# Two hybrid mixers on one core: narrow projection columns appended to wider units, and the second mixer's units reordered

## Chip, cores, metric

One core of one Trainium2 chip. The metric is the device time of one launch in microseconds (us); lower is better.

## What is computed

A stack of four layers on 256 tokens of width 1024, in float32. The two layers of the first kind are half a gated feed-forward block, a hybrid mixer and another half block; the two of the second kind are a hybrid mixer and a feed-forward block with squared ReLU; a norm ends the stack. Cut to the parts that matter here:

```python
def hybrid_mixer(h, w_in, ...):                       # first kind, two layers
    dn_qkv, dn_z, dn_b, dn_a, sb_q, sb_k, sb_v, gate_a, gate_b = split_cols(h @ w_in)
    ...
    beta = jax.nn.sigmoid(dn_b.astype(jnp.float32)).transpose(0, 2, 1)
    g = (-jnp.exp(a_log.astype(jnp.float32))
         * jax.nn.softplus(dn_a.astype(jnp.float32) + dt_bias.astype(jnp.float32))).transpose(0, 2, 1)

def hybrid_layer(x, positions, g_mix, w_in, ...):     # second kind, two layers
    h = rms_norm(x, g_mix)
    (a_q, a_k, a_v, b_qlat, b_kvlat, b_krope,
     c_q, c_k, c_v, c_f, d_val, d_gate) = jnp.split(h @ w_in, split_points, axis=-1)
    ...
    k_rot = apply_rope(b_krope, positions)
    log_f = jax.nn.log_sigmoid(c_f.astype(jnp.float32) + b_forget.astype(jnp.float32))
```

Three outputs of the projections are narrow: `dn_b` and `dn_a` together (16 columns), `c_f` (4 columns) and `b_krope` (32 columns). The three attentions of the second mixer have four heads each.

## The kernel before

**Units.** All weights are read as units of 2048 numbers on each of 128 partitions: 1024 rows by 256 columns (as eight chunks of 128 rows), or 256 rows by 1024 columns. SP loads a unit into one of three `raw` buffers; ScalarE rounds it into `whi` (`split_hi`), VectorE writes the rest into `wlo` (`split_lo`); TensorE multiplies in three products, high by high, high by low and low by high (`product3`). A buffer's next load waits for `lo_done`, its next rounding for `multiplied`. Each engine's program is written out by hand, unit after unit; on ScalarE and VectorE the split of unit n+2 stands ahead of the work on unit n's result.

**Two layouts.** In `feature_product` the weights are stationary and the 256 tokens move: the result has features on the rows, 48 products of 256 columns a unit. In `row_unit` (the value units `sv`, `av`, `cv`) the tokens are stationary, 128 at a time, and the weights move: the result has tokens on the rows.

**Borders.** A mixer begins at a border: the last rows of the block before are added to x (L424), squared (L519 to L531), the scale is taken (L535), x scaled (L550, L556) and turned by TensorE (`norm_pe`, L573); chunk by chunk ScalarE writes `xhi` (L546) and VectorE `xlo` (L561), and `chunk_ready` holds TensorE until a chunk has both. VectorE splits the mixer's first unit ahead of the border.

**First mixer** (`mix1_*`): 28 projection units (`IN1`, from `sk` 0), then gates, branches and output. Ahead of unit 0 the 16 columns are multiplied by themselves, `ba_hi` and `ba_lo` stationary, the 256 tokens moving, chunk by chunk (24 products); the 16-row result is copied (L1097), turned back in two transposes (L964) and copied again, and `small_act_1` and `small_dve_1` work on it at unit 2, the cumulative sum follows at unit 4.

**Second mixer** (`mix2_*`): ten projection units (`IN2`), 16 gate units, four branch units, four output units. The 4 columns of `c_f` are multiplied ahead of unit 0 in the same way (`cf_hi`, `cf_lo`). The 160 columns of `b_kvlat` and `b_krope` are taken as one unit, bkv, whose two products overlap by 64 columns. Latent norms, up projections and the rotary turn follow at fixed units. Head i of the twelve has its scores on TensorE at the end of unit 7 + i (`HEAD2_AT`), its maximum on VectorE and its exponential on ScalarE at 8 + i, its weights scaled by VectorE (L2326 to L2329) and turned by TensorE (L2097) at 9 + i, its values at 10 + i. VectorE's rotary steps (`rope_dve`, L2289 to L2301) stand in unit 7, `mask_rows_dve` in unit 8, `sums_dve` in unit 10, and the 31 taps of a convolution (L2413, L2415) are spread over the units by `TAPS_AT`.

```python
TAPS_AT = {7: 4, 8: 4, 9: 4, 10: 3, 11: 3, 12: 3, 13: 2, 14: 2, 15: 2, 16: 2, 17: 1, 18: 1}
```

Of the kernel before, what the change touches and what calls it, by code (L numbers as in the profile page):

```python
# [6 lines left out]
F32 = mybir.dt.float32  # L7
# [27 lines left out]
ARENA = 19840  # L35
# [25 lines left out]
def constants():  # L61
# [5 lines left out]
    for s in range(LOW, LEVELS):  # L67
        parts[f"level{s}"] = (r >> (s + 1) == c >> (s + 1)) & (c >> s & 1 == 1) & (r >> s & 1 == 0)
    b = np.arange(BLK)
# [11 lines left out]
def constants_2():  # L81
# [12 lines left out]
    parts = {"ones2": np.ones((P, T)), "causal": np.where(r > c, MASKED, 0.0),  # L94
# [13 lines left out]
def hybrid_stack_kernel(nc, d, out):  # L108
    ctx = ExitStack()
    with ctx:  # L110
# [8 lines left out]
        raw = [sb(f"raw{s}", [P, UNIT]) for s in range(SLOTS)]  # L119
        whi = [sb(f"whi{s}", [P, UNIT], F32R) for s in range(SLOTS)]  # L120
        wlo = [sb(f"wlo{s}", [P, UNIT], F32R) for s in range(SLOTS)]
# [41 lines left out]
        small = sb("small", [P, 256])  # L163
        later_keys = sb("later_keys", [P, 384])
        ba_w = (sb("ba_raw", [P, KC, 16]), sb("ba_hi", [P, KC, 16], F32R), sb("ba_lo", [P, KC, 16], F32R))
# [10 lines left out]
        def as_in(w):  # L176
            return w[:].rearrange("p (c n) -> p c n", c=KC)

        def as_out(w):
            return w[:].rearrange("p (c n) -> p c n", c=2)  # L180
# [45 lines left out]
        tensor_waited = sem("tensor_waited")  # L226
# [61 lines left out]
        def split_lo(e, n):  # L288
            s, r = n
            e.wait_ge(hi_done[s], r)  # L290
            e.wait_ge(raw_in[s], r * 16)
            e.tensor_tensor(wlo[s][:], raw[s][:], whi[s][:].bitcast(F32), ALU.subtract).then_inc(lo_done[s], 1)  # L292
# [479 lines left out]
        def ffn1_dve(e, l, r0, u0, j, f):  # L772
# [59 lines left out]
            split_lo(e, unit(r0, u0 + U_FFN1))  # L832
# [9 lines left out]
        N1 = len(IN1)  # L842
        CONV = [n for n in range(N1) if IN1[n][0] in ("q", "k", "v")]
# [28 lines left out]
        ba_turn = sg[0][0:16, 0:T]  # L872
# [4 lines left out]
        ba_raw, ba_hi, ba_lo = ba_w  # L877

        def ev(name, per):
# [4 lines left out]
            ba_hi_done=1, ba_lo_done=1, ba_product=1, ba_copied=1, ba_turned=1, ba_kept=1, exp_b=1, one_b=1, beta_done=1, a_shift=1, abs_a=1,  # L884
# [12 lines left out]
        V["ba_lo_done"].start = 1  # L897
# [4 lines left out]
        def mix1_sync(e, l, r0, u0):  # L902
# [5 lines left out]
            e.wait_ge(V["ba_lo_done"].sem, 1 + l)  # L908
            e.dma_start(ba_raw[:], w[l, :, BA_COL:BA_COL + 16].rearrange("(c p) n -> p c n", p=P)).then_inc(ba_in.sem, 16)
            for n in range(N1):  # L910
                kind, g = IN1[n]
                load_unit(e, unit(r0, u0 + n), columns(w, KIND_COL[KINDS.index(kind)] + g * 256), as_in, True)
# [24 lines left out]

        def head_at(n, after):

            return HEAD_AT.index(n - after) if n - after in HEAD_AT else None  # L940

        def mix1_pe(e, l, r0, u0, j):
            norm_pe(e, j)

            e.wait_ge(*V["ba_hi_done"](l))
            e.wait_ge(*V["ba_lo_done"](l))
            for c in range(KC):
                chunk_ready(e, j, c)
                mm = product3(e, bank[4][0:16, 0:T], ba_hi[:, c, :], ba_lo[:, c, :], xhi[:, c, :], xlo[:, c, :],
                              c == 0, c == KC - 1)  # L950
            mm.then_inc(V["ba_product"].sem, 1)
            for n in range(N1 + TAIL):
                if n < N1:
                    if n >= 2:
                        kept_unit(e, l, n - 2)
                    if IN1[n][0] == "sv":
# [3 lines left out]
                if n == 1:  # L960
                    e.wait_ge(*V["ba_copied"](l))
                    e.sem_inc(tensor_waited)
                    for t in range(TT):
                        mm = e.transpose(bank[4][:, t * 16:(t + 1) * 16], ba_turn[:, t * P:(t + 1) * P], ident[0:16, 0:16])  # L964
                    mm.then_inc(V["ba_turned"].sem, 1)
                if n == 4:
# [102 lines left out]
        def keep_unit_act(e, l, r0, u0, n):  # L1069
            kind, g = IN1[n]  # L1070
            wait_unit(e, r0, u0, n)
            if n in CONV:
# [3 lines left out]
                e.activation(pre[i % 2][:, :, 3:3 + T], b2(n % 2), ACT.Copy).then_inc(V["pre_copied"].sem, 1)  # L1076
            elif kind == "sv":
                e.activation(sv[:, :, g * 256:(g + 1) * 256], b2(n % 2), ACT.Copy).then_inc(V["kept"].sem, 1)
            else:
                e.activation(home(n), bank[n % 2][:], ACT.Copy).then_inc(V["kept"].sem, 1)  # L1080

        def mix1_act(e, l, r0, u0, j):
            split_hi(e, unit(r0, u0))
            e.wait_ge(ba_in.sem, l * 16 + 16)
            e.wait_ge(multiplied[(u0 - 4) % SLOTS], r0 + (u0 - 4) // SLOTS + 1)
            e.activation(ba_hi[:], ba_raw[:], ACT.Copy).then_inc(V["ba_hi_done"].sem, 1)
            norm_act(e, j, lambda c: col("mix_norm", l, c), unit(r0, u0 + 1))
            for n in range(N1 + TAIL):
# [4 lines left out]
                if n + 2 <= N1 + 1:  # L1093
                    split_hi(e, unit(r0, u0 + n + 2))
                if n == 0:
                    e.wait_ge(*V["ba_product"](l))
                    e.activation(ba_turn, bank[4][0:16, 0:T], ACT.Copy).then_inc(V["ba_copied"].sem, 1)  # L1097
# [4 lines left out]
                if n == 5:  # L1102
# [5 lines left out]
                if n == 2:  # L1108
# [81 lines left out]
        def mix1_dve(e, l, r0, u0, j):  # L1190
            e.wait_ge(*V["ba_hi_done"](l))
            e.tensor_tensor(ba_lo[:], ba_raw[:], ba_hi[:].bitcast(F32), ALU.subtract).then_inc(V["ba_lo_done"].sem, 1)
            xlo_dve(e, j, lambda c: col("mix_norm", l, c))
            split_lo(e, unit(r0, u0 + 1))
            for n in range(N1 + TAIL):
# [12 lines left out]
                if n + 2 <= N1 + 1:  # L1208
# [5 lines left out]
                if n == 5:  # L1214
# [29 lines left out]
                if n == 2:  # L1244
# [61 lines left out]
        def small_act_1(e, l):  # L1306
            e.wait_ge(*V["ba_turned"](l))
            e.activation(ba, bank[4][:, 0:32], ACT.Copy).then_inc(V["ba_kept"].sem, 1)
            e.wait_ge(*V["ba_kept"](l))
# [375 lines left out]
        def mix1_delta_dve(e, l, r0, u0):  # L1685
# [27 lines left out]
            for s in range(LOW, LEVELS):  # L1713
                mask = const(f"level{s}").unsqueeze(1).to_broadcast([P, 4, P])
                last = s == LEVELS - 1
                for g in range(GROUPS):
                    e.wait_ge(*V["m_product"](l, (s - LOW) * 4 + g))
                    if last:
                        e.tensor_tensor(Mb[g][:, :, 64:P], b4(g)[:, :, 64:P], mask[:, :, 64:P], ALU.mult)\
# [72 lines left out]
        CF_COL = 1952  # L1792
# [7 lines left out]
        TAPS_AT = {7: 4, 8: 4, 9: 4, 10: 3, 11: 3, 12: 3, 13: 2, 14: 2, 15: 2, 16: 2, 17: 1, 18: 1}  # L1800
# [22 lines left out]
        cf_turn = rtmp[0:H2, 0:T]  # L1823
# [9 lines left out]
        def const2(name):  # L1833
# [5 lines left out]
        cf_raw, cf_hi, cf_lo = [w[:, :, 0:H2] for w in ba_w]  # L1839
# [7 lines left out]
            cf_hi=1, cf_lo=1, cf_product=1, cf_copied=1, cf_turned=1, cf_kept=1, cf_abs=1, cf_exp=1, cf_ln=1, lf=1,  # L1847
# [10 lines left out]
        def mix2_sync(e, l, r0, u0, j):  # L1858
            w = d["w_in_2"]

            def columns(w, c):
# [4 lines left out]
            e.dma_start(ba_w[0][:, :, 0:H2], w[l, :, CF_COL:CF_COL + H2].rearrange("(c p) n -> p c n", p=P))\  # L1866
             .then_inc(small_in, 16)
# [4 lines left out]
            for n in range(10):  # L1872
                load_unit(e, unit(r0, u0 + n), columns(w, IN2_COL[IN2[n]]), as_in, True)
# [78 lines left out]
        def mix2_pe(e, l, r0, u0, j):  # L1952
            norm_pe(e, j)
            e.wait_ge(*W["cf_hi"](l))
            e.wait_ge(*W["cf_lo"](l))
            for c in range(KC):
                chunk_ready(e, j, c)
                mm = product3(e, bank[4][0:H2, 0:T], cf_hi[:, c, :], cf_lo[:, c, :], xhi[:, c, :], xlo[:, c, :],
                              c == 0, c == KC - 1)
            mm.then_inc(W["cf_product"].sem, 1)  # L1960
            for n in range(B2):
# [5 lines left out]
                if n < G2 and IN2[n] in ("av", "cv"):  # L1967
# [745 lines left out]
```

## Time and profile before

| | us |
|---|---|
| three timed runs | 2390.36, 2391.69, 2392.84 (median 2391.69) |
| the profiled execution: span, first to last instruction | 2391.4 |
| mixers of the first kind start (first product behind the border) | 209.3 and 966.6 |
| mixers of the second kind start | 1534.8 and 1962.7 |

The page gives the profiled execution's span and no other time for it; the span agrees with the timed runs within their spread. Times in a timeline are us from the start of the span, then the duration. A matmul's record is longer than its pitch, because the next begins while it still drains, so the pitch is read from one start to the next. A bracket at the end of a row gives the idle time of the engine before it and what ended it.

### The profile page before, as it was taken

How to read it: one execution, taken by the hardware profiler on the slowest of the kernel's cores; microseconds unless marked ns; L12 is line 12 of the kernel's file. 1: busy time of each engine (PE TensorE's matmuls, PEld its weight loads, DVE VectorE, ACT ScalarE, POOL GpSimd, SP SyncE). 2: the span in 40 equal slices, each digit the busy share in tenths (PEclk: the TensorE clock that was granted, in tenths of full speed). 3: DMA queues.
4: the chain of work that ended last, by engine and by line, in shares of the span. 5: the costliest groups of instructions: out<-in, count | busy, mean ns of one | idle time of the engine just before them, and what ended most of it. 6: DMA issues, size and time to landing. Idle time of an engine off the chain costs nothing. (4 is left out here: it accounts for less than half of the span.)

```text
span 2391.4 us, 40848 instructions
## 1 busy us (share of the span) xinstructions
PE 2351.3 (98%) x17170; PEld 2214.4 (93%) x17170; DVE 1589.6 (66%) x1952; ACT 1402.6 (59%) x1872; POOL 145.8 (6%) x119
## 2 busy tenths in 40 slices
PE   8999999999999999999999999999999999999998
PEld 7998999999999999899999999899999989999998
DVE  5666668856666756667875666659785455978554
ACT  5455778555555545678845655546754455675443
POOL 0000002200000000001400000000030000004000
PEclk9999999999999999999999999999999999999999
DMA  6555544235555556444415556544455654455653
GB/s 227 195 177 160 159 138 145 72 124 174 179 194 176 188 182 193 146 147 134 141 54 167 181 168 207 184 125 136 147 177 190 195 184 139 127 156 168 204 183 123
DMA packets 312453, 386.57 MB, mean 162 GB/s; under 512 B 10812, under 2 KB 287440, under 8 KB 312272
## 3 DMA queue, kind: packets, MB, share of 16 engines
q1 hardware_dynamic: 312160, 383.91, 49.8%
q8 instruction: 136, 2.23, 0.4%
q14 instruction: 45, 0.37, 0.0%
q10 hardware_dynamic: 112, 0.06, 0.0%
HBM read 382.89 MB, written 1.06 MB: 161 GB/s over the span
## 5 line engine op out<-in xcount | busy, mean ns | idle before, releaser
L313 PE MATMUL bank<-xhi,whi 128*128 128x256 f32 x3712 | 1064.8, 287 | 4.1 <-DVE wlo L302 4.1
L315 PE MATMUL bank<-xhi,wlo 128*128 128x256 f32 x3712 | 1052.3, 283 | 0.0
L314 PE MATMUL bank<-xlo,whi 128*128 128x256 f32 x3712 | 1052.2, 283 | 0.0
L292 DVE TENSOR_TENSOR wlo<-raw,whi 128x2048 fp32r<-128x2048 f32 x354 | 817.3, 2311 | 205.9 <-ACT whi L276 204.1
L276 ACT ACTIVATE whi<-raw 128x2048 fp32r<-128x2048 f32 x355 | 676.5, 1907 | 204.7 <-PE bank L315 204.7
L313 PEld LDWEIGHTS bank<-xhi,whi 128*128 128x128 f32 x3712 | 714.2, 192 | 9.3 <-DVE wlo L302 4.2
L314 PEld LDWEIGHTS bank<-xlo,whi 128*128 128x128 f32 x3712 | 714.3, 192 | 4.8 <-issue 1.9
L315 PEld LDWEIGHTS bank<-xhi,wlo 128*128 128x128 f32 x3712 | 713.7, 192 | 0.0
L313 PE MATMUL bank<-whi,yhi 128*128 128x512 f32 x608 | 237.9, 391 | 0.0
L314 PE MATMUL bank<-wlo,yhi 128*128 128x512 f32 x608 | 237.4, 390 | 0.0
L315 PE MATMUL bank<-whi,ylo 128*128 128x512 f32 x608 | 236.6, 389 | 0.0
L792 DVE TENSOR_TENSOR arena<-bank,arena 128x512 f32<-128x512 f32 x44 | 30.4, 691 | 210.3 <-PE bank L315 210.1
L315 PEld LDWEIGHTS bank<-whi,ylo 128*128 128x128 f32 x608 | 114.2, 188 | 24.3
L313 PEld LDWEIGHTS bank<-whi,yhi 128*128 128x128 f32 x608 | 114.5, 188 | 22.6 <-issue 0.9
L314 PEld LDWEIGHTS bank<-wlo,yhi 128*128 128x128 f32 x608 | 114.4, 188 | 21.0
L711 ACT ACTIVATE arena<-arena 128x512 f32<-128x512 f32 x44 | 27.8, 632 | 168.8 <-DVE arena L792 168.8
L2561 DVE SCALAR_TENSOR_TENSOR arena<-bank,arena 128x512 f32<-128x512 f32 x32 | 22.1, 692 | 149.5 <-PE bank L315 145.3
L1067 POOL TENSOR_TENSOR arena<-arena 128x512 f32<-128x512 f32 x32 | 46.1, 1441 | 1053.1 <-ACT arena L1057 1053.1
L313 PE MATMUL bank<-yhi,whi 128*128 128x256 f32 x384 | 109.0, 284 | 0.0
L314 PE MATMUL bank<-ylo,whi 128*128 128x256 f32 x384 | 108.7, 283 | 0.0
L315 PE MATMUL bank<-yhi,wlo 128*128 128x256 f32 x384 | 108.7, 283 | 0.0
L313 PE MATMUL bank<-whi,xhi 128*128 128x256 f32 (+1 forms) x320 | 105.7, 330 | 0.2
(407 smaller groups left out, 2944.3 us busy)
## 6 DMA issues: line engine op xcount, KB each, us to landing
raw<-in_w_in SPq DMA_DIRECT2D x92, 1024.0 KB, 5.2
raw<-in_ffn_w_in SPq DMA_DIRECT2D x88, 1024.0 KB, 5.1
raw<-in_ffn_w_out SPq DMA_DIRECT2D x44, 1024.0 KB, 5.0
raw<-in_w_gate SPq DMA_DIRECT2D x32, 1024.0 KB, 5.6
raw<-in_w_up SPq DMA_DIRECT2D x32, 1024.0 KB, 5.4
raw<-in_w_down SPq DMA_DIRECT2D x32, 1024.0 KB, 4.9
raw<-in_w_branch_b SPq DMA_DIRECT2D x8, 1024.0 KB, 5.1
raw<-in_w_branch_a SPq DMA_DIRECT2D x8, 1024.0 KB, 5.4
```

Of the source, the lines that this page charges most:

```text
L276: e.activation(whi[s][:], raw[s][:], ACT.Copy).then_inc(hi_done[s], 1)
L292: e.tensor_tensor(wlo[s][:], raw[s][:], whi[s][:].bitcast(F32), ALU.subtract).then_inc(lo_done[s], 1)
L313: e.matmul(o, ahi, bhi, start=start, stop=False, skip_group_check=True)
L314: e.matmul(o, ahi, blo, start=False, stop=False, skip_group_check=True)
L315: return e.matmul(o, alo, bhi, start=False, stop=stop, skip_group_check=True)
L711: e.activation(eg, gbuf, ACT.Abs).then_inc(gate_act, 1)
L792: e.tensor_tensor(two(gbuf), two(gate_of(i)[:]), spread_two(), ALU.mult).then_inc(gate_dve, 1)
L1067: e.tensor_tensor(home(n), home(n), sg[m % 2], ALU.mult).then_inc(V["silu"].sem, 1)
L2561: e.scalar_tensor_tensor(two(eg), two(gate_of(i)[:]), 0.0, spread_two(), ALU.max, ALU.mult)\
```

## The change

**First mixer.** The 16 columns become columns 256 to 271 of the first value unit (`BA_AT`, unit 3): a second load brings them into the same buffer, the splits of this unit run over 272 columns a chunk, and `wide_unit` multiplies with tokens on the rows, each half of the tokens into a bank of its own. The 16 columns then have tokens on the rows and need no turning. Unit 0 takes the chunks as they come (`first_unit`: both halves of its columns per chunk). `small_*_1` moves to unit 3, the cumulative sum to unit 5, `small_*_2` to unit 6.

**Second mixer.** The value unit cv moves from the last of ten to the first; `c_f` lies beside it in memory and comes with its load (260 columns), `b_krope` by a second load (32 columns): 292 columns, tokens on the rows, chunk by chunk behind the border. The last 96 columns are turned in two transposes, so that `b_krope` has features on the rows. bkv becomes a unit of 128 columns. All other units move back by one; the steps tied to them move too, the rotary, mask and sum steps on VectorE included, and the taps start at unit 8. `HEAD2_AT` and `CHAIN_AT` stay.

The buffers of slot 0 grow to 2336 columns; constants, the arena and `small` shrink to make room.

```diff
-ARENA = 19840
+ARENA = 19712
+WIDE_1, WIDE_2 = 256 + 16, 256 + 4 + 32
...
+        room = [KC * WIDE_2, UNIT, UNIT]
+        raw = [sb(f"raw{s}", [P, room[s]]) for s in range(SLOTS)]
...
-        def split_hi(e, n):
+        def split_hi(e, n, size=UNIT):
...
-            e.activation(whi[s][:], raw[s][:], ACT.Copy).then_inc(hi_done[s], 1)
+            e.activation(whi[s][:, 0:size], raw[s][:, 0:size], ACT.Copy).then_inc(hi_done[s], 1)
...
+        def first_unit(e, n, o, j):
...
+            for c in range(KC):
+                chunk_ready(e, j, c)
+                for b in range(2):
+                    mm = product3(e, o[:, b * T:(b + 1) * T], as_in(whi[s])[:, c, b * P:(b + 1) * P],
+                                  as_in(wlo[s])[:, c, b * P:(b + 1) * P], xhi[:, c, :], xlo[:, c, :],
+                                  b == 0 and c == 0, c == KC - 1)
...
+        def wide_unit(e, n, outs, width, j=None):
...
+            for t in range(TT):
+                for c in range(KC):
+                    if j is not None and t == 0:
+                        chunk_ready(e, j, c)
+                    mm = product3(e, outs[t][:, 0:width], xhi[:, c, t * P:(t + 1) * P], xlo[:, c, t * P:(t + 1) * P],
+                                  as_in(whi[s], width)[:, c, :], as_in(wlo[s], width)[:, c, :], c == 0, c == KC - 1)
...
-            e.wait_ge(*V["ba_hi_done"](l))
-            e.wait_ge(*V["ba_lo_done"](l))
-            for c in range(KC):
-                chunk_ready(e, j, c)
-                mm = product3(e, bank[4][0:16, 0:T], ba_hi[:, c, :], ba_lo[:, c, :], xhi[:, c, :], xlo[:, c, :],
-                              c == 0, c == KC - 1)
-            mm.then_inc(V["ba_product"].sem, 1)
...
-        IN2 = ("bq", "bkv", "dval", "dgate", "aq", "ak", "av", "cq", "ck", "cv")
+        IN2 = ("cv", "bq", "bkv", "dval", "dgate", "aq", "ak", "av", "cq", "ck")
...
-        TAPS_AT = {7: 4, 8: 4, 9: 4, 10: 3, 11: 3, 12: 3, 13: 2, 14: 2, 15: 2, 16: 2, 17: 1, 18: 1}
+        TAPS_AT = {8: 4, 9: 4, 10: 4, 11: 3, 12: 3, 13: 3, 14: 2, 15: 2, 16: 2, 17: 2, 18: 2}
...
-                    for b in range(2):
-                        for c in range(KC):
-                            mm = product3(e, bank[n % 2][:, b * T:(b + 1) * T], as_in(whi[s])[:, c, b * 64:b * 64 + P],
-                                          as_in(wlo[s])[:, c, b * 64:b * 64 + P], xhi[:, c, :], xlo[:, c, :],
-                                          c == 0, c == KC - 1)
+                    for c in range(KC):
+                        mm = product3(e, bank[n % 2][:, 0:T], as_in(whi[s], P)[:, c, :], as_in(wlo[s], P)[:, c, :],
+                                      xhi[:, c, :], xlo[:, c, :], c == 0, c == KC - 1)
...
-                if n == 7:
+                if n == 8:
                     rope_dve(e, l)
-                if n == 8:
+                if n == 9:
                     mask_rows_dve(e, l)
-                if n == 10:
+                if n == 11:
                     sums_dve(e, l)
...
             if l < DEPTH - 1:
-                split_lo(e, unit(r0, u0 + U_FFN2))
+                e.wait_ge(krope_in, (l + 1) * 16 + 16)
+                split_lo(e, unit(r0, u0 + U_FFN2), KC * WIDE_2)
```

**What moves on the engines.** TensorE, start of the second mixer in layer 0, before (rows by columns of the result; the names behind the arrow are what moves and what is stationary; `x16` are the transposes of the border):

```order
L573 MATMUL bank<-table,arena 128x128 x16
L313 MATMUL bank<-xhi,ba_hi 4x256
L314 MATMUL bank<-xlo,ba_hi 4x256
L315 MATMUL bank<-xhi,ba_lo 4x256
L313 MATMUL bank<-xhi,ba_hi 4x256
```

And with the change:

```order
L576 MATMUL bank<-table,arena 128x128 x16
L316 MATMUL bank<-whi,xhi 128x292
L317 MATMUL bank<-wlo,xhi 128x292
L318 MATMUL bank<-whi,xlo 128x292
L316 MATMUL bank<-whi,xhi 128x292
```

The 24 products with four stationary columns are gone, and the wide unit, its weights moving, stands directly behind the transposes.

VectorE in the second mixer, around the maximum of head 0 (TENSOR_REDUCE of a score bank), before; the rows on `rotary` are the rotary turn, those on `dw` the taps, `wlo<-raw,whi` a split:

```order
L2296 TENSOR_TENSOR arena<-bank,rotary 32x256
L2297 TENSOR_TENSOR arena<-arena,rotary 32x256
L2299 TENSOR_TENSOR arena<-arena 32x256
L2301 COPY arena<-arena 32x1024
L2413 TENSOR_SCALAR arena<-arena,dw,cols 128x256 x2
L2415 SCALAR_TENSOR_TENSOR arena<-arena,dw 128x256 x6
L2335 TENSOR_REDUCE small<-bank 128x1
L2336 TENSOR_REDUCE small<-bank 128x1
L2338 TENSOR_SCALAR small<-small 128x2
L292 TENSOR_TENSOR wlo<-raw,whi 128x2048
L1915 MEMSET arena 2x8x64
L1917 TENSOR_SCALAR arena<-arena 2x4x64 x2
```

And with the change (its lines are some 35 higher):

```order
L294 TENSOR_TENSOR wlo<-raw,whi 128x2048
L2369 TENSOR_REDUCE small<-bank 128x1
L2370 TENSOR_REDUCE small<-bank 128x1
L2372 TENSOR_SCALAR small<-small 128x2
L294 TENSOR_TENSOR wlo<-raw,whi 128x2048
L2325 TENSOR_TENSOR arena<-bank,rotary 32x512
L2326 TENSOR_TENSOR arena<-arena,rotary 32x512
L2328 TENSOR_TENSOR arena<-arena 32x512
L2325 TENSOR_TENSOR arena<-bank,rotary 32x512
L2326 TENSOR_TENSOR arena<-arena,rotary 32x512
L2328 TENSOR_TENSOR arena<-arena 32x512
L2332 TENSOR_TENSOR arena<-bank,rotary 32x256
```

The maximum of head 0 stood behind the rotary steps and four taps; now it stands ahead of them, behind the split of unit 9 alone.

SP's queue at the second mixer of layer 0, before:

```order
L1866 DMA ba_raw<-in_w_in 128x8x4
L1868 DMA arena<-in_w_uq 128x2x384
L1869 DMA arena<-in_w_ukv 128x512
L1871 DMA arena<-bias_rows 128x4x256
L270 DMA raw<-in_w_in 128x8x256 x10
```

And with the change:

```order
L1893 DMA arena<-in_w_uq 128x2x384
L1894 DMA arena<-in_w_ukv 128x512
L1896 DMA arena<-bias_rows 128x4x256
L272 DMA raw<-in_w_in 128x8x260
L1902 DMA raw<-in_w_in 128x8x32
L272 DMA raw<-in_w_in 128x8x256
L272 DMA raw<-in_w_in 128x8x128
L272 DMA raw<-in_w_in 128x8x256 x7
```

The load of 4 columns is gone from its place ahead of the others; a load of 32 columns follows the first unit's.

## Rows read from the trace of the kernel before

**Rows 1.** The page: busy us, share of the span and instructions of each engine
```profile
PE 2351.3 (98%) x17170; PEld 2214.4 (93%) x17170; DVE 1589.6 (66%) x1952; ACT 1402.6 (59%) x1872; POOL 145.8 (6%) x119
```

**Rows 2.** Waits of TensorE, whole span: us in total, times, longest us
```profile
PE bank L2097 <- DVE arena L2329: 7.9, 4, 2.1
...
PE bank L974 <- ACT arena L1117: 0.5, 2, 0.3
```

**Rows 3.** Timeline (start us, us, engine line, op), first mixer of layer 0, its start
```profile
208.63 3.23 DVE L561 SCALAR_TENSOR_TENSOR xlo<-bank,cols,xhi 128x256 fp32r<-128x256 f32 x8 [0.33 <-ACT xhi L546]
...
209.26 0.28 PE L313 MATMUL bank<-xhi,ba_hi 128*16 128x256 f32 x1 [0.41 <-DVE xlo L561]
...
212.13 2.29 DVE L292 TENSOR_TENSOR wlo<-raw,whi 128x2048 fp32r<-128x2048 f32 x1 [0.27 <-ACT whi L283]
...
212.35 0.28 PE L313 MATMUL bank<-xhi,whi 128*128 128x256 f32 x1
...
213.78 0.28 PE L313 MATMUL bank<-xhi,whi 128*128 128x256 f32 x1
```

**Rows 4.** Timeline of TensorE, the unit ahead of the same border: products of 512 columns
```profile
199.07 0.39 PE L314 MATMUL bank<-wlo,yhi 128*128 128x512 f32 x1
...
201.79 0.39 PE L314 MATMUL bank<-wlo,yhi 128*128 128x512 f32 x1
```

**Rows 5.** Timeline of TensorE, first mixer: turning the 16 rows back
```profile
223.95 0.23 PE L964 MATMUL bank<-table,arena 16*128 16x16 f32 x1
```

**Rows 6.** Timeline of TensorE, second mixer's starts; busy by stretch (clock behind POOL)
```profile
1534.76 0.28 PE L313 MATMUL bank<-xhi,ba_hi 128*4 128x256 f32 x1 [0.41 <-DVE xlo L561]
...
1539.11 0.28 PE L313 MATMUL bank<-xhi,whi 128*128 128x256 f32 x1
...
1962.66 0.28 PE L313 MATMUL bank<-xhi,ba_hi 128*4 128x256 f32 x1 [0.41 <-DVE xlo L561]
...
1965.76 0.28 PE L313 MATMUL bank<-xhi,whi 128*128 128x256 f32 x1
...
1535.10:1538.50 3.40, 3.40 (x18) 1.99 (x17) 3.13 (x7) 3.40 (x7) 0.00 (x0) 0.50 0.00 0
```

**Rows 7.** Timeline of VectorE and ScalarE ahead of the second mixer's borders
```profile
1522.45 1.90 ACT L276 ACTIVATE whi<-raw 128x2048 fp32r<-128x2048 f32 x1
...
1524.38 2.29 DVE L292 TENSOR_TENSOR wlo<-raw,whi 128x2048 fp32r<-128x2048 f32 x1 [1.11 <-ACT whi L276]
...
1526.59 1.88 DVE L424 SCALAR_TENSOR_TENSOR x<-bank,x 128x512 f32<-128x512 f32 x3
...
1954.41 2.05 DVE L424 SCALAR_TENSOR_TENSOR x<-bank,x 128x512 f32<-128x512 f32 x3 [0.67 <-PE bank L315]
```

**Rows 8.** Timeline of VectorE and TensorE in the second mixer of layer 0, the attention heads
```profile
1590.10 2.29 DVE L292 TENSOR_TENSOR wlo<-raw,whi 128x2048 fp32r<-128x2048 f32 x1 [2.73 <-ACT whi L276]
...
1596.61 0.36 PE L313 MATMUL bank<-xhi,whi 128*128 128x256 f32 x1
...
1607.45 3.63 DVE L2415 SCALAR_TENSOR_TENSOR arena<-arena,dw 128x256 f32<-128x256 f32 x8
...
1651.93 0.35 DVE L2329 TENSOR_SCALAR arena<-arena,small 128x256 f32<-128x256 f32 x1
...
1653.78 0.27 PE L2097 MATMUL bank<-table,arena 128*128 128x128 f32 x1
```

**Rows 9.** Loads (count, KB each, median us to landing), and timeline of SP and ScalarE
```profile
raw<-in_w_in SPq DMA_DIRECT2D x92, 1024.0 KB, 5.2
...
ba_raw<-in_w_in SPq DMA_DIRECT2D x2, 64.0 KB, 5.3
...
200.95 0.37 SPq L270 DMA_DIRECT2D raw<-in_w_in  x1
...
1939.34 3.64 SPq L270 DMA_DIRECT2D raw<-in_w_in  x2
...
1949.51 1.90 ACT L276 ACTIVATE whi<-raw 128x2048 fp32r<-128x2048 f32 x1
```

More of the change, by code:

```diff
@@ L93, in constants_2 @@
     freq[64:96, 0] = np.tile(inv_freq, 2)
-    parts = {"ones2": np.ones((P, T)), "causal": np.where(r > c, MASKED, 0.0),
+    parts = {"ones2": np.ones((P, 64)), "causal": np.where(r > c, MASKED, 0.0),
              "turn": turn, "freq": freq, "flip": r + c == P - 1,
@@ L286, in split_hi_half, with split_lo @@
             return up
-        def split_lo(e, n):
+        def split_lo(e, n, size=UNIT):
             s, r = n
@@ L831, in ffn1_dve @@
                 tables_dve(e)
-            split_lo(e, unit(r0, u0 + U_FFN1))
+            if l == DEPTH - 1 and u0:
+                e.wait_ge(krope_in, 16)
+                split_lo(e, unit(r0, u0 + U_FFN1), KC * WIDE_2)
+            else:
+                split_lo(e, unit(r0, u0 + U_FFN1))
             border_dve(e, unit(r0, u0 + 32), 0.5, j)
@@ L959, in mix1_pe @@
                         feature_product(e, unit(r0, u0 + n), bank[n % 2], xhi, xlo)
[L960 to L966, printed above, removed]
+                if n == BA_AT + 2:
                     e.wait_ge(*V["g_done"](l))
@@ L1076, in keep_unit_act @@
                 e.activation(pre[i % 2][:, :, 3:3 + T], b2(n % 2), ACT.Copy).then_inc(V["pre_copied"].sem, 1)
+            elif n == BA_AT:
+                for t, o in enumerate((bank[n % 2], bank[4])):
+                    e.activation(ba[:, t * 16:(t + 1) * 16], o[:, 256:WIDE_1], ACT.Copy)
+                    up = e.activation(sv[:, t, 0:256], o[:, 0:256], ACT.Copy)
+                up.then_inc(V["kept"].sem, 1)
             elif kind == "sv":
@@ L1966, in mix2_pe @@
                         e.wait_ge(*W["g_kept"](l, n - 2 - G2))
-                if n < G2 and IN2[n] in ("av", "cv"):
+                if n == 0:
+                    wide_unit(e, unit(r0, u0), (bank[4], bank[5]), WIDE_2, j)
+                elif n < G2 and IN2[n] == "av":
                     row_unit(e, unit(r0, u0 + n), bank[n % 2], xhi, xlo)
@@ L2078, in scores_pe @@
             if i < 4:
-                e.wait_ge(*W["kept"](l, 5))
+                e.wait_ge(*W["kept"](l, KEPT2("ak")))
             elif i < 8:
@@ L2123, in head_scale, with size2 @@
             return 96.0 ** -0.5 if i // 4 == 1 else 1.0
+        def size2(n):
+            return KC * P if n < G2 and IN2[n] == "bkv" else UNIT
         def mix2_act(e, l, r0, u0, j):
-            split_hi(e, unit(r0, u0))
-            e.wait_ge(small_in, l * 64 + 64)
-            e.activation(cf_hi, cf_raw, ACT.Copy).then_inc(W["cf_hi"].sem, 1)
+            e.wait_ge(krope_in, l * 16 + 16)
+            split_hi(e, unit(r0, u0), KC * WIDE_2)
             norm_act(e, j, lambda c: col("g_mix_2", l, c), unit(r0, u0 + 1))
@@ L2235, in keep_unit2_act @@
             src = bank[n % 2][:]
-            if n >= G2:
+            if n == 0:
+                for t in range(TT):
+                    up = e.activation(tail[:, t, :], bank[4 + t][:, WIDE_2 - 96:WIDE_2], ACT.Copy)
+                up.then_inc(W["tail_kept"].sem, 1)
+                for t in range(TT):
+                    up = e.activation(cv[:, t, :], bank[4 + t][:, 0:256], ACT.Copy)
+                up.then_inc(W["kept"].sem, 1)
+            elif n >= G2:
                 k = n - G2
@@ L2245, in keep_unit2_act @@
                 e.activation(dpad[:, :, CONV_K - 1:], b2(n % 2), ACT.Copy).then_inc(W["kept"].sem, 1)
+            elif IN2[n] == "bkv":
+                e.activation(bkv[:, 0, :], src[:, 0:T], ACT.Copy).then_inc(W["kept"].sem, 1)
             elif IN2[n] == "dgate":
@@ L2662, in _ @@
         def _(e):
-            for s in (*lo_done, gated, hlo_done, V["ba_lo_done"].sem):
+            for s in (*lo_done, gated, hlo_done):
                 e.sem_inc(s)
```

174 lines of the change are left out of this document (91 added, 83 removed).

## The prediction

> **What bounds the kernel now.** I read the page's busy shares first: TensorE is busy 98% of a span of 2391.4 us [rows 1]. That alone proves little, so the second view is TensorE's waits: the longest in total is 7.9 us over the whole program, in four places where the softmax weights of the second mixer are turned (L2097, for VectorE) [rows 2]. TensorE's row of matmuls is therefore the path, nearly everywhere, and a matmul taken out of it is worth its pitch (start to start, not the duration of the record, since matmuls overlap), as long as VectorE, ScalarE and the loads keep the next unit ready. So the questions are: what is the pitch of what goes and of what comes, and where does TensorE, arriving earlier, have to wait.
>
> Pitches. Twelve products of 256 columns run from 212.35 to 213.78: 0.119 us each [rows 3]. Twelve of 512 columns run from 199.07 to 201.79: 0.227 us each [rows 4]. Between the two a column costs (0.227 - 0.119) / 256 = 0.42 ns.
>
> **The change part by part**, against the profiled execution (its span 2391.4; the median of the timed runs, 2391.69, is 0.3 us above it, within their spread of 2390.36 to 2392.84).
>
> 1. *The narrow product of the first mixer goes.* In layer 0 it runs from 209.26 to 212.35, where the first unit begins: 3.09 us for 24 products, because each chunk waits for VectorE's residues, which come at 3.23/8 = 0.40 us per chunk [rows 3]. Now the first unit itself goes chunk by chunk, six products a chunk, 0.72 us against 0.40, so it never waits after the first chunk and starts at what was 209.26. The next unit must then be split at 209.26 + 48 x 0.12 = 215.0; VectorE starts that split at 212.13 and is through at 214.4 [rows 3]. 0.6 us to spare: nothing added. Layer 1 is the same program: 2 x -3.09 = **-6.2**.
>
> 2. *The columns come back as width.* 48 products of 272 and 48 of 292 columns in each layer, in place of 256. No row has these widths. The ends are the 256 price (no cost) and the 512 price (192 products x 0.108 = 20.6 us). I take the line between them, since both widths lie next to 256 and the two rows differ only in columns: 48 x 16 x 0.42 ns = 0.32 and 48 x 36 x 0.42 ns = 0.73 a layer, together **+2.1**. The Trainium skill (TensorE: Matmul & The Clock Gate, "Back-to-back issue gap") gives sustained pitches of 81 ns at 128 columns and 131 ns at 512, an estimate of 0.13 ns a column; by it this term would be 0.7 and the total 1.4 us lower; the trace, with 227 ns at 512 columns, does not agree.
>
> 3. *Transposes and small steps of the first mixer.* The two transposes of the 16-row result go: 0.23 us [rows 5], twice, **-0.5**. The 0.25 us that the norm's column sum waits for ScalarE in each layer [rows 2] comes from ScalarE standing behind the small steps in unit 2; they now stand at unit 3, whose VectorE part has no convolution taps, and I count the wait as gone: **-0.5**. In the second mixer two transposes go and two come: nothing.
>
> 4. *The narrow product of the second mixer goes.* In layer 1 it takes 1962.66 to 1965.76, 3.10 us; in layer 0 1534.76 to 1539.11, 4.35 us, because the granted clock there is 0.50 (1.2 GHz) for 3.4 us, after a border in which TensorE had stood idle and then ran in short pieces [rows 6]. Sum -7.45. The wide unit that takes its place needs three products of 0.134 = 0.40 us per chunk in its first pass, just the pace of the residues, so it is neither held nor helped. The border is the same, so I let the same 3.4 us at half clock fall on it: 1.7 us. Together **-5.75**. If no low stretch falls there it is 1.7 better; if one falls on layer 1's border too, 1.7 worse.
>
> 5. *The latent unit (bkv) does 24 products in place of 48*: 24 x 0.119 = 2.86 us, twice, **-5.7**. What this could uncover is the split of the next units: when unit n-1 ends, ScalarE copies it out and splits unit n+2, 1.9 us and 2.3 on VectorE [rows 7]; TensorE comes for it two units later, now 2.9 + 5.8 = 8.7 us at the shortest. Covered, with some 4 us left for the copy and the small steps.
>
> 6. *The first split of the second mixer grows from 2048 to 2336 columns.* It stands ahead of the border on both engines. In layer 0 VectorE starts it at 1524.38, when ScalarE is through, and goes at 1526.59 into the border's first sum without a pause, so the border starts as late as the split ends [rows 7]: 288/2048 of 1.90 us on ScalarE and of 2.29 on VectorE, 0.27 + 0.32, **+0.6**. In layer 1 VectorE waits 0.67 us there [rows 7], which hides it.
>
> 7. *VectorE in the attention part: the term I am least sure of.* The units move back by one, the heads do not: head 0's scores still follow unit 7. On VectorE the rotary steps and the first four taps, which ran before the maximum of head 0, now stand behind it. The maximum waits for head 0's scores, which end about 1596.6, where the next unit starts; VectorE's run without a pause began at 1590.10, after a wait of 2.73 us [rows 8]. So the same work starts 6.7 us later against TensorE. In return the split of unit 9 lies ahead of the wait (2.25 us) and, up to head 5's weights, two taps fewer are ahead of them (a tap is 3.63/4 = 0.9 us; 1.8 us). Head 5's weights were ready at 1652.3 and TensorE took them at 1653.78 [rows 8]; they would be ready at 1652.3 + 6.7 - 2.25 - 1.8 = 1654.95, 1.2 us too late. Earlier heads lose less, having more taps fewer ahead of them, and later ones have as many taps as before, so the delay stays and doesn't add up: **+2.4** for two layers. The waits of today [rows 2] may move to other heads; they are part of this account, which compares when TensorE takes the weights. Ends: nothing, and the whole 6.7 us a layer.
>
> 8. *Loads.* A load of 1024 KB lands in 5.2 us and the narrow one in 5.3 [rows 9]. In the first mixer both are issued at 200.95 or just after [rows 9] and are wanted when ScalarE has kept unit 0, which ends at 215.0: 10.5 us of 14. In layer 1 of the second mixer the load is issued at 1939.34 and wanted at 1949.51 [rows 9]: 10.2, tight if the two landings add up, easy if they overlap. I take nothing.
>
> Sum: -6.2 + 2.1 - 1.0 - 5.75 - 5.7 + 0.6 + 2.4 = -13.5. From the median: 2391.7 - 13.5 = **2378.2 us**.
>
> **Rivals.**
> *Nothing is given back*: VectorE catches up in the attention part and no low clock falls on the wide unit. For it: VectorE still waits 2.73 us before 1590.10 [rows 8], so it has some room there, and layer 1's border shows no low clock (3.10 us, as in the first mixer [rows 6]). -13.5 - 2.4 - 1.7 = -17.6, 2374.1.
> *VectorE becomes the bound in the attention part.* If the 6.7 us later start is not made good at all, each layer loses 6.7 in place of 1.2: -13.5 + 11.0 = -2.5, 2389.2. Against it: the split and the taps are certainly out of its way.
> *The narrow loads hold the split.* The split of the wide units now waits for a second load, in pieces of 64 or 128 bytes, behind the large one. The row of the narrow load gives 5.3 us at 64-byte pieces, as a load of 1024 KB has 5.2 [rows 9], so the price of small pieces hardly shows at this size. If, behind a large load, it took twice that, the last border would be held by 10.5 + 5.3 - 10.2 = 5.6 us: 2383.8. The Trainium skill (DMA: Bandwidth & Descriptors, "Specifications") asks for at least 512 bytes in a transfer for line rate, which speaks for this rival; no row here shows a narrow load behind a large one.
> *Slower: a width above 256 is priced as 512.* Then term 2 is 20.6 in place of 2.1, +18.5, 2396.7. It decides from a pitch of 0.119 + (13.5 + 2.1) / 192 = 0.20 us in the wide units. For it: no row shows a width between the two; against it: the cost per column between 256 and 512 (0.42 ns) is just one column per cycle at 2.4 GHz, which leaves no room for a step.
> That the change does not do what it says is excluded: the order of TensorE shows the narrow products gone.
>
> **How the numbers follow.** Forecast 0.68, its own range 2375.5 to 2382 (low clock at either border, 0 to 2.5 us a layer for VectorE). Nothing given back 0.12, VectorE bound 0.10 (half of it nearer the middle), narrow loads 0.05, width priced as 512 0.05. The range, 2374 to 2385, takes in the first rival and leaves out most of the others. A measurement of this kernel can tell about 0.2% (4.8 us) from no change: faster 0.90, same 0.05, slower 0.05.
>
> **What would show it.** Right: the first unit of each first mixer starts where the narrow product did, right behind the border; 292-column products at a pitch of 0.134 to 0.136; the latent unit in 2.9 us; the waits at the turning of the softmax weights about 1 us more in sum per layer, or moved to later heads. Wrong: a pitch near 0.2 in the wide units; a wait of the wide split for the narrow load; waits of over 5 us more at the turned weights in each layer; units of the second mixer held by their splits.

## The result and the profile after

The changed kernel takes **2371.29 us** (median; 2371.13 to 2372.5) against 2391.58 us (2390.36 to 2392.84) in the same comparison: a ratio of 0.9914, 95% interval 0.9901 to 0.9928, or 20.3 us less. The prediction was 2378.2 us with a range down to 2374: the sign and most of the mechanism were right, the size was not. The profiled execution has a span of 2370.7 us (2391.4 before); a launch's time is 1.8 us above its span in these runs.

The page of the changed kernel, busy us of each engine, answers to [rows 1]:

```profile
PE 2327.5 (98%) x17022; PEld 2191.8 (92%) x17022; DVE 1587.2 (67%) x1948; ACT 1402.8 (59%) x1874; POOL 144.0 (6%) x119
```

TensorE is still busy 98%: it stayed the path. Its waits (us in total, times, longest us), to be read beside [rows 2]; the lines of the code have moved, L2097 is now L2124 and L974 is L1000:

```profile
PE bank L2124 <- DVE arena L2363: 11.1, 7, 3.1
...
PE bank L576 <- DVE arena L559: 6.4, 4, 1.6
...
PE bank L316 <- DVE arena L2474: 1.2, 2, 0.6
...
PE bank L576 <- DVE arena L553: 0.7, 1, 0.7
```

The turned softmax weights now cost 11.1 us in place of 7.9, and the norm's column sum (L974 in [rows 2]) is no longer in the list. New are 0.7 us at one border (L553) and two waits of 0.6 us for the branch products of the second mixer (L2474).

The timeline of TensorE at the places of [rows 3] and [rows 6]: start us, us, line, operands (the moving one first), shape, idle time before it.

```profile
208.01 0.35 PE L316 MATMUL bank<-xhi,whi 128*128 128x256 f32 x1 [0.41 <-DVE xlo L564]
...
225.17 0.29 PE L316 MATMUL bank<-whi,xhi 128*128 128x272 f32 x1
...
231.19 1.02 PE L1000 MATMUL bank<-arena,table 128*128 128x512 f32 x2
...
1521.79 0.59 PE L316 MATMUL bank<-whi,xhi 128*128 128x292 f32 x1
...
1529.33 0.28 PE L316 MATMUL bank<-xhi,whi 128*128 128x256 f32 x1
...
1537.86 0.38 PE L2011 MATMUL bank<-table,arena 128*96 128x128 f32 x2
...
1946.48 0.38 PE L316 MATMUL bank<-whi,xhi 128*128 128x292 f32 x1 [0.41 <-DVE xlo L564]
...
1953.02 0.28 PE L316 MATMUL bank<-xhi,whi 128*128 128x256 f32 x1
```

The first unit of the first mixer starts straight behind the border, with the same idle time of 0.41 us that stood ahead of the narrow product. The 272-column unit takes 6.02 us (0.1254 a product), the 292-column unit 7.54 us in layer 0 and 6.54 in layer 1.

But the first row says something else too. In the kernel before, this point came at 209.26 [rows 3], 1.25 us later, and TensorE's work ahead of it is the same; the diff changes the size of some buffers there. 0.3 us of the 1.25 are an earlier first weight product (14.61 us against 14.92). To see where the rest comes from, take one block of the first feed-forward part in both traces: 96 products of 256 columns, then 24 of 512, then the next block. Kernel before:

```profile
113.90 0.28 PE L313 MATMUL bank<-xhi,whi 128*128 128x256 f32 x1
...
125.41 0.40 PE L313 MATMUL bank<-whi,yhi 128*128 128x512 f32 x1
...
130.88 0.28 PE L313 MATMUL bank<-xhi,whi 128*128 128x256 f32 x1
```

Changed kernel:

```profile
112.95 0.28 PE L316 MATMUL bank<-xhi,whi 128*128 128x256 f32 x1
...
124.34 0.39 PE L316 MATMUL bank<-whi,yhi 128*128 128x512 f32 x1
...
129.86 0.28 PE L316 MATMUL bank<-xhi,whi 128*128 128x256 f32 x1
```

11.51 us against 11.39 for the same 96 products, and 5.47 against 5.52 for the same 24; the blocks from 46 to 180 us repeat these numbers to 0.01 us. Over the whole program the mean start to start of neighbouring products at full clock is 119.89 ns before and 118.63 after at 256 columns, 227.76 and 229.91 at 512. With 12,960 products of the one kind before (12,624 after) and 2,208 of the other that is many microseconds, and the prediction has no term for it.

### The profile page after: what moved, and what is told of

Its sections match the earlier page's. It is cut to its first block and busy times, and to the rows that moved or that the text cites. A ratio compares the mean times of both kernels' runs of the same rounds, so it can differ in the third digit from the quotient of the medians.

```text
span 2370.7 us, 40537 instructions
## 1 busy us (share of the span) xinstructions
PE 2327.5 (98%) x17022; PEld 2191.8 (92%) x17022; DVE 1587.2 (67%) x1948; ACT 1402.8 (59%) x1874; POOL 144.0 (6%) x119
## 5 line engine op out<-in xcount | busy, mean ns | idle before, releaser
L317 PE MATMUL bank<-xlo,whi 128*128 128x256 f32 x3696 | 1041.4, 282 | 0.0
L316 PEld LDWEIGHTS bank<-xhi,whi 128*128 128x128 f32 x3696 | 702.4, 190 | 10.3 <-DVE wlo L305 4.2
L317 PEld LDWEIGHTS bank<-xlo,whi 128*128 128x128 f32 x3696 | 700.5, 190 | 5.0 <-issue 1.9
L318 PEld LDWEIGHTS bank<-xhi,wlo 128*128 128x128 f32 x3696 | 700.2, 189 | 0.0
L316 PE MATMUL bank<-whi,xhi 128*128 128x256 f32 (+3 forms) x320 | 107.3, 335 | 1.6 <-DVE arena L2474 1.2
```

Of the source, the lines that this page charges most:

```text
L316: e.matmul(o, ahi, bhi, start=start, stop=False, skip_group_check=True)
L317: e.matmul(o, ahi, blo, start=False, stop=False, skip_group_check=True)
L318: return e.matmul(o, alo, bhi, start=False, stop=stop, skip_group_check=True)
```

## The experiments

**Theory 1**: the missing gain comes from the addresses. The change makes slot 0's three buffers 9344 bytes long in place of 8192 (288 columns more), so everything laid out behind them moves. **Theory 2**: the addresses do nothing, and the changed mixers save more than was counted.

### Before's program in the change's layout (b_layout), and the reverse (a_aligned)

```diff
-        raw = [sb(f"raw{s}", [P, UNIT]) for s in range(SLOTS)]
+        room = [2336, UNIT, UNIT]
+        raw_room = [sb(f"raw{s}", [P, room[s]]) for s in range(SLOTS)]
...
+        raw, whi, wlo = [[w[:, 0:UNIT] for w in r] for r in (raw_room, whi_room, wlo_room)]
...
-        ba_w = (sb("ba_raw", [P, KC, 16]), sb("ba_hi", [P, KC, 16], F32R), sb("ba_lo", [P, KC, 16], F32R))
+        ba_w = [r[0][:, UNIT:UNIT + KC * 16].rearrange("p (c n) -> p c n", c=KC) for r in (raw_room, whi_room, wlo_room)]
```

> The kernel before with the change's memory layout alone: slot 0's three buffers are 2336 columns wide, the narrow weights live in their last columns, the arena, the small block and two tables shrink as in the change; not one instruction of TensorE is added, removed or moved. Theory 1 (the gain that was not predicted comes from the addresses: the products of 256 columns run at 0.1186 us start to start in the changed kernel and at 0.1199 before, also in the feed-forward parts whose code is the same): 7 to 11 us faster than before, 2380 to 2385 us, 256-column pitch 0.1186 to 0.1188, 512-column pitch 0.230. Theory 2 (the addresses do nothing, the changed mixers save more than was counted): 2391 to 2392 us, pitch 0.1199 and 0.228.

In the changed kernel, the order in which the buffers are laid out: raw0 and whi0, each followed by small tables that fill its place up to 16384 bytes, then raw1, raw2, whi1, whi2, wlo1, wlo2, x, xhi, xlo, yhi, ylo, wlo0, and the rest.

> The changed kernel with its buffers laid out anew: every weight buffer and every activation buffer begins a multiple of 8 KB from the first one, as in the kernel before (in the changed kernel they are displaced by multiples of 1152 bytes); the program is the same. Theory 1: the 256-column pitch goes back to 0.1199 and the time up by 7 to 11 us, 2378 to 2382 us. Theory 2: 2371 to 2372 us, pitch 0.1186 as now.

Measured: b_layout 2384.97 us, ratio 0.9965 (0.9954 to 0.9977) to the kernel before; a_aligned 2380.42 us, ratio 0.9948 (0.9934 to 0.9963). The same block, in b_layout and then in a_aligned:

```profile
113.63 0.28 PE L316 MATMUL bank<-xhi,whi 128*128 128x256 f32 x1
...
125.02 0.39 PE L316 MATMUL bank<-whi,yhi 128*128 128x512 f32 x1
...
130.54 0.28 PE L316 MATMUL bank<-xhi,whi 128*128 128x256 f32 x1
```

```profile
113.44 0.28 PE L320 MATMUL bank<-xhi,whi 128*128 128x256 f32 x1
...
124.96 0.40 PE L320 MATMUL bank<-whi,yhi 128*128 128x512 f32 x1
...
130.43 0.28 PE L320 MATMUL bank<-xhi,whi 128*128 128x256 f32 x1
```

The pitch goes with the layout and not with the program: 11.39 and 5.52 us in b_layout, 11.52 and 5.47 in a_aligned. Theory 2 falls. The ratios add up: the layout alone is worth 0.0035 x 2391.6 = 8.4 us (5.5 to 11.0), the change in an aligned layout 0.0052 x 2391.6 = 12.4 us (8.8 to 15.8), together 20.8 beside the 20.3 measured. VectorE and ScalarE do not explain it: in the kernel before the 256-column pitch is 120.0 ns with both idle and 119.9 with both splitting weights, in b_layout 118.4 and 118.6.

### Which addresses (b_gap, b_wlo128, b_x128, b_all128)

Each is the kernel before with one empty buffer laid out between others:

```diff
+        gap = sb("gap", [P, 128])
         x = sb("x", [P, TT, D])
```

> The kernel before with 512 bytes left empty between the weight buffers and the activations, nothing else. If the distance between a product's two operands is what counts (a part of theory 1): the pitch of the 256-column products falls below 0.1199 and the time by 3 to 11 us. If it is the distance among the three weight slots, or the place of the arena's many small operands, or theory 2: 2390 to 2392.5 us and a pitch of 0.1199.

Measured: 2391.47 us, ratio 0.9997 (0.9988 to 1.0007), 119.89 and 227.78 ns: nothing. I read this as the distance between weights and activations being out of it; the next runs show that this was wrong.

The other three move 128 bytes (`[P, 32]`): ahead of `wlo`, ahead of `x`, and ahead of `whi`.

> The kernel before with 128 bytes left empty between the high weight halves (whi) and the low ones (wlo), so that low weights and activations lie 128 bytes further; nothing else. Theory 1a (what counts is that whi and wlo, which follow one another as a product's operand, stand a multiple of 8 KB apart): the pitch of the 256-column products falls from 119.9 ns to 118 to 119 ns and the 512-column pitch rises from 227.8 to about 230, some 7 us of gain in all. Theory 1b (it is the distance of weights and activations, at less than the 512 bytes that were tried): no change here, 119.9 ns.

> The kernel before with 128 bytes left empty between the weight buffers and the activations, nothing else. Theory 1a (distance of whi and wlo): 119.9 ns, 227.8 ns, no change of the time. Theory 1b (distance of weights and activations, below 512 bytes): 118 to 119 ns and some 7 us of gain.

> The kernel before with 128 bytes left empty between the raw weights and everything that TensorE reads: its operands keep their distances and all begin 128 bytes later. Theory 1a and 1b: 119.9 ns, no change. Theory 1c (the place of each operand by itself, not a distance, sets the pitch): 118 to 119 ns.

Measured, one run each, beside 2391.58 (2390.3 to 2393.93 in seven runs): b_wlo128 2381.0 us (118.41 and 229.23 ns), b_x128 **2397.36 us** (119.01 and 232.44), b_all128 2391.23 (119.91 and 227.77). Theory 1c falls: moving all operands together does nothing, so it is a matter of distances. This run also moves the arena with its many small operands by the same 128 bytes as b_wlo128, so their place is not the cause. 1a has its number, as the block in b_wlo128 shows:

```profile
112.79 0.28 PE L314 MATMUL bank<-xhi,whi 128*128 128x256 f32 x1
...
124.15 0.39 PE L314 MATMUL bank<-whi,yhi 128*128 128x512 f32 x1
...
129.65 0.28 PE L314 MATMUL bank<-xhi,whi 128*128 128x256 f32 x1
```

That is 11.36 and 5.50 us. But 1b is not dead either: 128 bytes between weights and activations do change the pitch, at 256 columns for the better and at 512 for the worse. Over the program these two nearly cancel (-11.4 and +10.3 us), so the pitch alone does not make this kernel slower (see the last section). The block in b_x128:

```profile
114.09 0.28 PE L314 MATMUL bank<-xhi,whi 128*128 128x256 f32 x1
...
125.61 0.40 PE L314 MATMUL bank<-whi,yhi 128*128 128x512 f32 x1
...
131.19 0.28 PE L314 MATMUL bank<-xhi,whi 128*128 128x256 f32 x1
```

5.58 us for the 24 products of 512 columns. Its 256-column block takes 11.52, as before: in the first feed-forward part the pitch is 119.8 ns, in the rest 118.9, so the offset between whole buffers is not all that counts, and what else does is open.

### The change with other offsets (a_wlo128, a_lo128, a_wlo512)

The order of a_aligned, but wlo1, wlo2, wlo0 behind ylo and behind 128 bytes of small buffers (in a_wlo512, 512 bytes); in a_lo128 xlo and ylo behind these again.

> The changed kernel with all its large buffers a multiple of 8 KB apart, but for the three low weight halves, which stand 128 bytes off; no instruction differs. If it is the step from whi to wlo between one product's weights and the next that shortens the pitch (theory 1a), and the distance of weights and activations that lengthens the 512-column products: 256 columns at 117.6 to 118.7 ns as with the same gap in the kernel before, 512 columns at 227 to 229 ns, and 2366 to 2370 us. If the gain needs low weights and activations at one offset (as they stood there): 119.9 ns and 2378 to 2381 us, as with everything aligned.

> The same, with the low halves of the activations (xlo, ylo) a further 128 bytes off, 256 bytes from the high halves. If a step between the moving operands counts as well: 256 columns below 117.6 ns and a time below that of the run with the low weights alone. If only the stationary operands count: the same within 1 us, or slower where the 512-column products suffer from the distance (230 to 232 ns, up to 9 us more).

> As the first of these three, with the low weights 512 bytes off in place of 128. If any step does: 117.6 to 118.7 ns and 2366 to 2370 us. If 512 bytes count as no step (as between weights and activations, where 512 bytes changed nothing): 119.9 ns and 2378 to 2381 us.

Measured, one run each, beside one run of 2393.85 of the kernel before: 2380.73 us (119.05 and 231.25 ns), 2380.82 (119.04 and 231.28), 2380.37 (119.90 and 227.69). The first two miss the expected time by over 10 us, so theory 1a falls too: the step from whi to wlo alone gives part of the short products' gain and takes most of it back on the long ones. What paid, in b_wlo128, is low weights and activations together, 128 bytes off the high weights. 512 bytes are as good as none here too.

### Later heads (a_heads8), and the best layout (a_both128, a_both256)

```diff
-        HEAD2_AT = 7
+        HEAD2_AT = 8
```

> The changed kernel with the twelve heads of the second mixer begun one unit later (after unit 8 in place of 7), so that the rotary steps and the first taps stand ahead of head 0's maximum on VectorE again, as before the change. If term 7 of the prediction is right (VectorE's later start in the attention part costs the changed kernel some 1.2 us a layer): TensorE's waits for the turned softmax weights fall from 11.1 us to 8 or 9 and the time from 2371.3 to 2368 to 2370 us. If those waits come from VectorE's whole load there, they move to other heads: 2371 to 2372 us. If the last head, now one unit later, is late for the branch products: over 2372 us.

Measured: 2371.03 us, ratio 0.9914 (0.9897 to 0.993), the changed kernel's own, and not the 2368 to 2370 us expected. Yet the wait did what was expected; waits of TensorE in a_heads8:

```profile
PE bank L2124 <- DVE arena L2363: 7.5, 4, 2.3
```

and in a_aligned, where the heads stand as in the change:

```profile
PE bank L2128 <- DVE arena L2367: 9.5, 8, 2.0
```

3.6 us of this waiting went, the waits for the branch products (L2474) grew by 0.7, and the profiled span is 2.1 us shorter (2368.6), although it holds 3.4 us more at half clock than the changed kernel's (below). The medians can't tell the two apart.

The last two kernels have the heads later and are laid out raw1, raw2, whi1, whi2, 128 (256) bytes of small buffers, wlo1, wlo2, x to ylo, wlo0.

> The changed kernel with the heads one unit later, and laid out as the kernel before was with the gap of 128 bytes that paid most there: high weights a multiple of 8 KB apart, low weights and activations 128 bytes off. If offsets within 512 bytes and nothing else set the pitch, it is that of that run: 118.4 ns at 256 columns (the changed kernel's own layout has 118.6), 229.2 ns at 512 (229.9), some 4 us in all, and 2364 to 2369 us. If the change's own displacements of the third slot (256 bytes) are worth as much: 2370 to 2372 us.

> The same with 256 bytes in place of 128. If any offset that is not a multiple of 512 bytes does the same: within 2 us of the run with 128. If the size of the offset counts: another pitch at 256 or 512 columns and another time; at the worst, with 256 bytes as good as none, 119.9 ns and 2378 to 2381 us.

Measured: a_both128 **2368.92 us** (2368.51 to 2371.7), ratio 0.9902 (0.9886 to 0.9919), 118.32 and 229.41 ns; a_both256 2378.36 us, ratio 0.994 (0.9926 to 0.9955), 119.88 and 227.69 ns. The two differ in nothing but those 128 bytes and the small buffers that fill them, and their runs do not overlap (2376.0 to 2379.17 for the second): this pair shows what the offset is worth most directly, 9.4 us. The first is the lowest median of all, but its interval overlaps that of the changed kernel. The second has the pitches of an aligned kernel again: 256 bytes count as none.

## Why the prediction was right and wrong

**What failed** is a step that the prediction did not write down. It took 0.119 and 0.227 us [rows 3, 4] as prices of 256 and 512 columns, and used them for every product on either side of the change; the larger buffers of slot 0 were costed at nothing. The pitch is a price of the columns *and* of where the operands lie, and the change moves all of them. This is worth 8.4 us by b_layout; without it, in a_aligned, the change gains 12.4 us (8.8 to 15.8), and the sum said 13.5.

That the 12.4 lie so near the 13.5 is in part luck: no low clock fell on the wide unit in a_aligned, where the sum had put 1.7 us, but its trace has 3.4 us more of it in all than the trace before, at other places.

How the 8.4 us come about can be estimated from b_layout's trace: 12,960 products of 256 columns at 1.27 ns less, -16.5; 2,208 of 512 columns at 2.18 ns more, +4.8; and more time at the lower clock. Outside the start of the program and its last 30 us the granted clock, read in stretches of 1 us, is 0.50 (1.2 GHz) for 13.7 us in the kernel before and for 20.5 us in b_layout; half of the difference is lost against full clock, so +3.4. Sum -8.3. The two traces' own spans differ by 6.9 us (2391.4 and 2384.5), so the sum is good to 1 or 2 us; its last term, from one execution each, is the weakest. In the changed kernel it is 23.9 us at half clock, 10.2 more than before. The profile in stretches, the granted clock behind the five busy times:

```profile
424.00:431.00 7.00, 7.00 (x38) 7.00 (x38) 6.83 (x9) 2.82 (x3) 5.98 (x5) 0.57 0.82 272
1619.00:1626.00 7.00, 5.60 (x22) 5.25 (x23) 6.83 (x16) 4.67 (x12) 0.00 (x0) 0.54 0.18 34
1520.00:1524.00 4.00, 3.71 (x17) 3.53 (x18) 3.47 (x10) 3.35 (x9) 0.00 (x0) 0.58 0.00 0
```

By stretches of 1 us the half clock around the first two lasts 6.8 us each, one in the first mixer's delta part with TensorE busy all the time, the other among the attention heads. The third lies on the last transposes of the border and the wide unit behind it.

The steps, by their numbers:

1. *First mixer's narrow product*: right. 208.01 is where the narrow product would have begun, and no wait follows it: 3.09 us a layer.
2. *Width*: right. 0.1254 us at 272 columns and 0.1345 at 292 in the changed kernel, 0.1261 and 0.1342 in a_aligned, where 0.1257 and 0.134 were expected. The estimate from the Trainium skill (TensorE: Matmul & The Clock Gate, "Back-to-back issue gap") of 0.13 ns a column does not agree: from 256 to 292 columns a_aligned's trace gives 0.40 ns. The rival that priced the width as 512 is out.
3. *Transposes and the wait at the column sum*: right; the wait is gone from the list.
4. *Second mixer's narrow product*: right for the changed kernel. The product went, and the half clock fell on layer 0's border again for 3.4 us, as assumed. The unit takes 7.54 us there and 6.54 in layer 1, which is 1.0 us; the border's last eight transposes take 1.69 us in place of 1.09, which is 0.6; 1.6 together, where 1.7 was put on the unit alone. In a_aligned there was none. The transposes in the changed kernel, then before:

```profile
1520.29 1.69 PE L576 MATMUL bank<-table,arena 128*128 128x128 f32 x8 [1.64 <-DVE arena L559]
...
1533.26 1.09 PE L573 MATMUL bank<-table,arena 128*128 128x128 f32 x8 [1.65 <-DVE arena L556]
```

5. *Latent unit*: right. 72 products in place of 96 take 8.53 us (1529.33 to 1537.86), 0.1185 each, and no wait for a split follows.
6. *Wide first split*: right. VectorE's part takes 2.59 us where it took 2.29 [rows 7], +0.30 where 0.32 was expected. On TensorE it shows as the new wait of 0.7 us at L553, where the term said 0.6:

```profile
1511.11 2.59 DVE L294 TENSOR_TENSOR wlo<-raw,whi 128x2336 fp32r<-128x2336 f32 x1 [1.41 <-ACT whi L278]
```

7. *Attention part*: right in kind and near in size. The waits for the turned weights grew by 3.2 us (1.6 in a_aligned) where 2.4 was expected, and a_heads8, which puts VectorE's old order against the units back, takes 3.6 away again. The later start was 6.5 us by its own rows (1590.10 to 1596.6), not 6.7. The rival with VectorE as the bound (13.4 us for both layers) is out.
8. *Loads*: right, hidden. The second mixer's two loads in the changed kernel, layer 0 and then layer 1, and the first mixer's narrow load (count, KB each, us to landing):

```profile
raw<-in_w_in SPq DMA_DIRECT2D x1, 1040.0 KB, 9.7
raw<-in_w_in SPq DMA_DIRECT2D x1, 128.0 KB, 9.8
...
raw<-in_w_in SPq DMA_DIRECT2D x1, 1040.0 KB, 6.1
raw<-in_w_in SPq DMA_DIRECT2D x1, 128.0 KB, 6.3
...
raw<-in_w_in SPq DMA_DIRECT2D x2, 64.0 KB, 5.1
```

A narrow load behind a large one lands at most 0.6 us after it, so the two landings overlap. The 9.7 us belong to the place more than to the change: the kernel before's large load there took 8.9 (6.1 in layer 1, as now):

```profile
raw<-in_w_in SPq DMA_DIRECT2D x1, 1024.0 KB, 8.9
```

The wide split of layer 1 starts on ScalarE at 1933.24, 10.2 us after the large load's issue at 1923.08 and 3.5 us after the narrow load, issued at 1923.49, has landed:

```profile
1933.24 2.15 ACT L278 ACTIVATE whi<-raw 128x2336 fp32r<-128x2336 f32 x1
```

The Trainium skill (DMA: Bandwidth & Descriptors, "Specifications") asks for 512 bytes in a transfer for line rate; no cost of the smaller pieces shows here, with 64 KB in 5.1 us and 128 KB right behind the large load. The rival of the narrow loads is out.

One reading was off without consequence: 1.8 us stand between span and time, so the profiled execution before would have taken some 2393.2 us, 1.5 above the median and not 0.3 below it.

So the lower end of the range, which came from the rival with nothing given back, was set by terms of the mixers alone. Even that rival's 17.6 us fall short of the 20.3 measured.

## What to carry to other kernels

A change that resizes a buffer moves every buffer behind it, and on a kernel that is bound by TensorE this can bring nearly as much as the change itself (here 8.4 us beside 12.4), or cost. Before reading a gain as the change's own, compare the pitch of products in a part that the diff doesn't touch; if it differs, run the old program in the new layout. Where operands are laid out by hand, their offsets to one another are a knob of their own to try.

## What the runs showed that was not expected

**The pitch of float32r products hangs on the offsets of the operands to one another: 128 bytes matter, 256 and 512 count as none.** The table has all kernels but a_heads8, whose layout is the change's (27.3 us at half clock); offsets are worked out from the buffers' sizes in the order they are laid out, pitches are means over some 12,500 and 2,100 pairs of neighbours at full clock, and the last column has the us at half clock in the one profiled execution. The kernel before lay between 2391.1 and 2393.9 us in the comparisons.

| kernel | whi, wlo, activations: offset mod 256 | 256 columns, ns | 512 columns, ns | us | us at half clock |
|---|---|---|---|---|---|
| before | 0, 0, 0 | 119.89 | 227.76 | 2391.58 | 13.7 |
| b_gap (512 bytes) | 0, 0, 0 | 119.89 | 227.78 | 2391.47 | 17.1 |
| b_all128 | 128, 128, 128 | 119.91 | 227.77 | 2391.23 (one run) | 17.1 |
| a_aligned | 0, 0, 0 | 119.86 | 227.78 | 2380.42 | 17.1 |
| a_wlo512 | 0, 0, 0 | 119.90 | 227.69 | 2380.37 (one run) | 17.1 |
| a_both256 | 0, 0, 0 | 119.88 | 227.69 | 2378.36 | 20.5 |
| b_layout | 0, 128, 128 (slot 0: 128, 0, 128) | 118.62 | 229.94 | 2384.97 | 20.5 |
| after | 0, 128, 128 (slot 0: 128, 0, 128) | 118.63 | 229.91 | 2371.29 | 23.9 |
| b_wlo128 | 0, 128, 128 | 118.41 | 229.23 | 2381.0 (one run) | 23.9 |
| a_both128 | 0, 128, 128 | 118.32 | 229.41 | 2368.92 | 30.7 |
| b_x128 | 0, 0, 128 | 119.01 | 232.44 | 2397.36 (one run) | 30.7 |
| a_wlo128 | 0, 128, 0 | 119.05 | 231.25 | 2380.73 (one run) | 20.5 |
| a_lo128 | 0, 128, 0 | 119.04 | 231.28 | 2380.82 (one run) | 27.3 |

With all operands at one offset the 256-column pitch is 119.9 ns, and the 512-column pitch 227.7, in all six such kernels, whichever the offset and the program. With 128 bytes between some of them the short products gain 0.8 to 1.6 ns and the long ones lose 1.5 to 4.7. Other offsets between these buffers were not tried. What in the chip makes it so is not shown: VectorE and ScalarE, idle or busy, hardly change the pitch (118.4 and 118.6 ns in b_layout), and the loads were not separated.

**The kernels with the faster pitch also spent more time at half clock, in the one trace that each has**: 14 to 21 us in the six kernels with one offset, 21 to 31 in the others. That this comes from the pitch is not shown, and single traces are a weak witness: a_wlo128 and a_lo128 have the same pitches and times within 0.1 us of each other, with 20.5 and 27.3 us. Half of that time counts as lost where TensorE is the path, so it belongs in the account. With it the account closes for b_wlo128 too: -12,960 x 1.48 ns + 2,208 x 1.47 ns + 5.1 = -10.8 us, -10.6 measured; and it gives the sign of b_x128: -11.4 + 10.3 + 8.5 = +7.4, +5.8 measured. In b_x128 the pitches alone give -1.1, so its loss, seen in one run, hangs on the half clock, and why it had so much of it is open.
